# A two-block network on one Trainium2 core: routing spread over two stages, row sums respaced, whole weight loads, tile-wise first units

## The chip, the cores and the metric

The kernel is one program on one core of a Trainium2 chip. The metric is the device time of one execution in microseconds (us). A core has a matrix engine (TensorE, PE in the profile), VectorE (DVE), ScalarE (ACT), GpSimd (POOL) and SyncE (SP), each with its own instruction queue, and 16 DMA engines. Engines wait for each other by semaphores.

## The reference

Two transformer-like blocks for 256 tokens of width 2048, all float32. The part of the first block around which most of the change lies is "peer", a mixture over 16384 experts: eight heads, sixteen experts a head.

```python
q = (hf @ w_q).reshape(T, PEER_HEADS, 2, PEER_DKEY // 2)
s1, s2 = q[:, :, 0] @ sub_k1.T, q[:, :, 1] @ sub_k2.T
v1, i1 = lax.top_k(s1, 16); v2, i2 = lax.top_k(s2, 16)
cand = (v1[..., :, None] + v2[..., None, :]).reshape(T, 8, 256)
sv, si = lax.top_k(cand, 16)
e1, e2 = take_along_axis(i1, si // 16), take_along_axis(i2, si % 16)
expert, gate = e1 * 128 + e2, softmax(sv)
a = gelu(einsum('cd,chkd->chk', x, exp_u[expert]))
out = einsum('chk,chkd->cd', gate * a, exp_v[expert])
```

Before it come adaLN conditioning, a state-space mixer and sparse attention; after it the second block (projections "z", "gate", "abc", "w_o", and a feed-forward "up" and "down"). A root-mean-square norm stands ahead of the peer_q, z and up projections.

## The kernel before, in words

All dense weights stream through `ring` as 333 units of 128 x 4096 float32 (2 MB), in the order of `STREAM`: early (68), w_out, peer_q (8 each), then u0, u1, v0, u2, v1, u3, v2, v3 (16 each), z (17), gate (24), abc, w_o (8), up, down (32). The unit is the clock of the program: positions inside u0 to v3 are counted 0 to 127 (u0 is 0 to 15, v0 32 to 47, v3 112 to 127).

From `SPLIT_0` on each float32 unit is split into two float16 parts: SyncE loads it into one of two raw slots, ScalarE's `hi` writes the high part, VectorE's `low` (line 1149) the rest, each for the first half (p0) and the second half (p1) of the unit. TensorE does three float16 matmuls (lines 570 to 572) a tile. The semaphores are `hi_done`, `split_half` (p0 split), `split_done` (p1 split), `half_used` and `w_used` (TensorE is through with the first half, the unit). `hi` for unit n + 2 starts when unit n's half is used. Before, SyncE loads a unit in two halves of 1 MB: the first waits for `split_half` of two units earlier, the second for `split_done`.

The experts are computed in two ways. For tokens 48 to 255 all experts are evaluated densely in four quarters: u-stages give the activations, and 13 route steps a quarter turn gates into a table by one-hot products. A step is `route` on TensorE (32 small matmuls), and on VectorE `gated` (line 1683), `hot` for the step after next (lines 1669, 1671, 1675) and `gated_low` (line 1689). Quarter 0 is routed in u1, 1 in v0, 2 in v1, 3 in v2; each must be done before its v-stage (v0, v1, v2, v3). For tokens 0 to 47, GpSimd gathers the rows of `exp_u` and `exp_v` with indirect DMAs, 1 MB each: 48 row sums on VectorE (`row_dot`, line 1617) and 48 row products on TensorE (line 623). `DOT_AT` and `PRODUCT_AT` give their positions; `DOT_AT` is spread evenly from 19 to 111. u rows have one buffer, so a gather waits for the sum before it; at each eighth sum 1 MB of activations is loaded too (`h_load`).

`select` turns the sixteen best keys into experts by look-ups: for both index lists a compare, a multiply and a sum over 8 x 16 x 16 = 2048 elements (lines 1562, 1565, 1567), in u0 and at the start of u1.

At the end of w_out, v3 and w_o stands a norm. TensorE sums squares (`stat_sum`, `two_sums`), ScalarE takes the root, VectorE the reciprocal, and `norm_split` gives the sixteen tiles of `h_act` one after the other. The first unit of the next stage runs on these tiles: `unit_a(..., before=...)` waits for tile k in its first half m = 0, then does the second half m = 1.

## Time and profile before

| | |
|---|---|
| median of three runs | 3316.49 us (3311.57 to 3316.68) |
| profiled execution | 3314.53 us |
| its span on the core | 3312.8 us |
| mean granted TensorE clock | 0.979 |
| read from HBM | 814.00 MB |

The span runs from the first to the last instruction. The rows further down are copied from the trace of the profiled execution; a row "A <- B" of a waits view means that engine A stood idle until B ended.

### The profile page before, as it was taken

How to read it: one execution, taken by the hardware profiler on the slowest of the kernel's cores; microseconds unless marked ns; L12 is line 12 of the kernel's file. 1: busy time of each engine (PE TensorE's matmuls, PEld its weight loads, DVE VectorE, ACT ScalarE, POOL GpSimd, SP SyncE). 2: the span in 40 equal slices, each digit the busy share in tenths (PEclk: the TensorE clock that was granted, in tenths of full speed). 3: DMA queues.
4: the chain of work that ended last, by engine and by line, in shares of the span. 5: the costliest groups of instructions: out<-in, count | busy, mean ns of one | idle time of the engine just before them, and what ended most of it. 6: DMA issues, size and time to landing. Idle time of an engine off the chain costs nothing.

```text
span 3312.8 us, 71370 instructions
## 1 busy us (share of the span) xinstructions
PE 3177.2 (96%) x31258; PEld 2827.9 (85%) x31258; DVE 2345.1 (71%) x2673; ACT 1253.7 (38%) x1132; POOL 378.0 (11%) x284
## 2 busy tenths in 40 slices
PE   7999999999899998999899999999999999999998
PEld 4777768799898997889899997888888788888887
DVE  8496145699999985698679876578667665555554
ACT  2000143444444344344444444444443444433332
POOL 0276000000011222122222100200000000000000
PEclk8899999999999999999999999999999999999999
DMA  9657795446577888888998875655555466566663
GB/s 411 248 208 307 292 378 218 156 179 234 196 274 280 322 302 350 288 305 314 349 318 316 339 268 186 201 194 201 194 200 198 171 202 198 199 202 202 203 200 116
DMA packets 105300, 821.55 MB, mean 248 GB/s; under 512 B 12394, under 2 KB 14458, under 8 KB 15552
## 3 DMA queue, kind: packets, MB, share of 16 engines
q1 hardware_dynamic: 86112, 700.49, 58.7%
q0 software_dynamic: 16656, 115.53, 9.1%
q8 instruction: 192, 3.15, 0.4%
q10 hardware_dynamic: 2304, 2.10, 0.2%
q14 instruction: 36, 0.29, 0.0%
HBM read 814.00 MB, written 4.06 MB: 247 GB/s over the span
## 4 chain that ended last, share of the span: by engine, by line
PE 66%; DVE 22%; DMA 7%; issue 3%; ACT 1%; POOL 0%; ACTq 0%; DVEq 0%; SPq 0%
PE psW L570 17%; PE psW L571 16%; PE psW L572 16%; DVE ring L1149 9%; PE psW L568 7%; DMA arena<-urow_dram,rs 4%; DVE arena L1617 2%; DMA ring<-wst_dram 2%; PE psM L694 1%; PE psW L694 1%; DVE arena L1671 1%; PE psM L848 1%; DVE dyn L1675 1%; DVE work L1675 1%; DMA proj<-vrow_dram,rs 1%
## 5 line engine op out<-in xcount | busy, mean ns | idle before, releaser
L1149 DVE SCALAR_TENSOR_TENSOR ring<-ring 128x2048 f16<-128x2048 f32 x526 | 1199.4, 2290 | 516.2 <-ACT ring L1976 514.6
L570 PE MATMUL psW<-h_act,ring 128*128 128x256 f16 (+1 forms) x5088 | 1356.7, 267 | 48.7 <-DVE ring L1149 29.6
L571 PE MATMUL psW<-h_act,ring 128*128 128x256 f16 (+1 forms) x5088 | 1356.6, 267 | 0.0
L572 PE MATMUL psW<-h_act,ring 128*128 128x256 f16 (+1 forms) x5088 | 1356.2, 267 | 0.0
L1976 ACT ACTIVATE ring<-ring 128x2048 f16<-128x2048 f32 x526 | 998.2, 1906 | 868.5 <-PE psW L572 728.1
L570 PE MATMUL psW<-arena,ring 128*128 128x208 f16 (+1 forms) x3072 | 798.1, 260 | 12.1 <-DVE ring L1149 9.3
L571 PE MATMUL psW<-arena,ring 128*128 128x208 f16 (+1 forms) x3072 | 797.8, 260 | 0.0
L572 PE MATMUL psW<-arena,ring 128*128 128x208 f16 (+1 forms) x3072 | 797.7, 260 | 0.0
L570 PEld LDWEIGHTS psW<-h_act,ring 128*128 128x128 f16 x5088 | 500.9, 98 | 116.9 <-DVE ring L1149 40.9
L572 PEld LDWEIGHTS psW<-h_act,ring 128*128 128x128 f16 x5088 | 502.1, 99 | 36.8
L571 PEld LDWEIGHTS psW<-h_act,ring 128*128 128x128 f16 x5088 | 501.3, 99 | 35.3
L570 PEld LDWEIGHTS psW<-arena,ring 128*128 128x128 f16 x3072 | 300.9, 98 | 51.8 <-DVE ring L1149 19.2
L571 PEld LDWEIGHTS psW<-arena,ring 128*128 128x128 f16 x3072 | 301.1, 98 | 11.9
L572 PEld LDWEIGHTS psW<-arena,ring 128*128 128x128 f16 x3072 | 301.1, 98 | 11.9
L568 PE MATMUL psW<-h_act,ring 128*128 128x256 f32 x896 | 202.8, 384 | 2.7 <-DVE h_act L1299 2.7
L568 PEld LDWEIGHTS psW<-h_act,ring 128*128 128x128 f32 x896 | 168.9, 191 | 32.2 <-issue 7.8
L2371 POOL DMA_INDIRECT arena<-urow_dram,rs x48 | 119.9, 2497 | 659.7 <-DVE rs L1617 657.9
L2197 ACT ACTIVATE arena<-work 128x512 f16<-128x512 f32 x52 | 32.8, 630 | 336.4 <-DVE work L1683 336.4
L1617 DVE CUSTOM_DVE_ANT_0 arena<-arena,proj 128x2048 f32<-128x2048 f32 x48 | 109.7, 2285 | 53.6 <-DMA arena<-urow_dram,rs 53.6
L2371 POOL DMA_INDIRECT proj<-vrow_dram,rs x48 | 88.2, 1838 | 87.6 <-PE psM L623 75.4
L694 PE MATMUL psW<-ring,csilu 128*32 128x256 f32 x832 | 64.3, 462 | 23.0 <-DVE small L1260 17.4
L694 PEld LDWEIGHTS psW<-ring,csilu 128*32 128x32 f32 x832 | 29.0, 128 | 51.8 <-issue 33.0
(391 smaller groups left out, 2531.3 us busy)
## 6 DMA issues: line engine op xcount, KB each, us to landing
ring<-wst_dram SPq DMA_DIRECT2D x522, 1024.0 KB
ring<-wst_dram SPq DMA_DIRECT2D x72, 2048.0 KB, 11.3
proj<-h_rows POOLq DMA_DIRECT2D x6, 1024.0 KB
x_res<-xT_dram POOLq DMA_DIRECT2D x2, 2048.0 KB, 17.6
out_dram<-x_res SPq DMA_DIRECT2D x4, 512.0 KB, 2.9
bias_rows<-proj POOLq DMA_DIRECT2D x1, 1536.0 KB, 21.9
x_res<-cmat_dram POOLq DMA_DIRECT2D x1, 1024.0 KB, 5.1
x_res<-bmat_dram ACTq DMA_DIRECT2D x8, 128.0 KB, 3.9
```

What stands on the lines that cost most here:

```text
L568: return nc.tensor.matmul(out, ring[:, w0:w0 + P], rhs, start=first, stop=last)
L570: nc.tensor.matmul(out, whi(s, col, P), xh, start=first, stop=False)
L571: nc.tensor.matmul(out, whi(s, col, P), xl, start=False, stop=False)
L572: return nc.tensor.matmul(out, wlo(s, col, P), xh, start=False, stop=last)
L694: mm = nc.tensor.matmul(ada_bank(n)[32 * c:32 * c + 32, 0:256], csilu[:, k:k + 1].to_broadcast([P, 32]), ring[:, s * UNIT + k * 256:s * UN ...
L848: mm = nc.tensor.matmul(psM[:, 2, 0:T], ring[:, s * UNIT + t * 512 + m * P:s * UNIT + t * 512 + (m + 1) * P], tiles(J, t), start=(t == 0), ...
L1149: ins = stt(wlo(s, c, n), ring[:, s * UNIT + c:s * UNIT + c + n], WSCALE, whi(s, c, n), ALU.mult, ALU.subtract)
L1617: v.tensor_tensor_reduce(row_buf[buf], row_buf[buf], h_rep, 1.0, 0.0, ALU.mult, ALU.add, dots[:, g, h:h + 1]).then_inc(dot_done, 1)
L1671: tt(hot2[b], iota16.unsqueeze(1).to_broadcast([P, STEP_T, P]), cols(1, P), ALU.is_equal).then_inc(hot2_ready, 1)
L1675: ins = tt(hot1[b][:, :, r, :], first1, gate, ALU.mult)
L1976: act(whi(s, p2 * (UNIT // 2), UNIT // 2), ring[:, c], ACT.Copy, scale=WSCALE).then_inc(hi_done, 1)
L2371: g.indirect_dma_start(row_buf[buf], None, (urow_d if kind == "u" else vrow_d)[:, :], bass.IndirectOffsetOnAxis(ap=row_index[:, i:i + 1], ...
```

## The change

1. `ROUTE_AT` and `route_steps` now give (quarter, step) by stage. Quarters 0 and 3 stay in u1 and v2. Quarter 1 takes positions 33 to 62 (v0 and u2), quarter 2 takes 65 to 94 (v1 and u3). Route steps by stage: v0 7, u2 6, v1 7, u3 6, where they were 13, 0, 13, 0.
2. `DOT_AT` starts at 22, goes on by 2.1, by 1.6 between 32 and 96, and by 3.0 after each eighth. It begins 22, 24, 26, 28, 30, 32, 34, 35, 38, 40, 41, 43, 45, 46, 48, 49, 52. Row sums by stage: u1 5 (7 before), v0 9 (8), u2 9 (8), v1 9 (9), u3 9 (8), v2 7 (8). The products follow.
3. The look-ups are done for ranks 0 to 7 over 8 candidates and for ranks 8 to 15 over 16.
4. From unit 72 on each unit is one DMA of 2 MB that waits for `split_done` of two units earlier.
5. The first unit of peer_q, z and up does both halves tile by tile (`first_unit`), the second into `psM`; `keep_clock` puts 12 and 32 matmuls whose result nobody reads around the sums of squares. The first half of the second unit is split ahead of the norm.

```diff
-ROUTE_AT = [14 * k // (STEPS - 1) for k in range(STEPS)]
-
-
-def route_steps(n):
-
-    return [k for k, at in enumerate(ROUTE_AT) if at == n]
-
-
 ORDER = ["u0", "u1", "v0", "u2", "v1", "u3", "v2", "v3"]
 
 
-DOT_AT = [19 + (i * (111 - 19)) // (ROWS_T - 1) for i in range(ROWS_T)]
+
+
+def route_at():
+
+    places = [range(16, 31), list(range(33, 48)) + list(range(48, 63)), list(range(65, 80)) + list(range(80, 95)), range(96, 111)]
+    return [(q, k, units[(len(units) - 1) * k // (STEPS - 1)]) for q, units in enumerate(places) for k in range(STEPS)]
+
+
+ROUTE_AT = route_at()
+
+
+def route_steps(name, n):
+
+    return [(q, k) for q, k, at in ROUTE_AT if at == 16 * ORDER.index(name) + n]
+
+
+def dots_at():
+
+    out, at = [], 22.0
+    for i in range(ROWS_T):
+        out.append(int(at))
+        at += 3.0 if i % HEADS == HEADS - 1 else 1.6 if 32 <= at < 96 else 2.1
+    return out
+
+
+DOT_AT = dots_at()
...
-            def load_halves(u, s, rank):
-
-                for p2, free in enumerate((split_half, split_done)):
-                    c = slice(p2 * HALF, (p2 + 1) * HALF)
-                    sp.wait_ge(free, rank - 1)
-                    sp.dma_start(ring[:, s * UNIT + p2 * HALF:s * UNIT + (p2 + 1) * HALF],
-                                 wst[u, :, c] if isinstance(u, int) else wst[u, :, c].rearrange("o p n -> (o p) n"))\
-                      .then_inc(raw_full[s][p2], 16)
+            def loads(a, b, free, less):
+
+                if a % 2:
+                    sp.wait_ge(free, a - less)
+                    load(a, 1)
+                    a += 1
+                with sp.Fori(a // 2, b // 2) as i:
+                    for s in range(2):
+                        sp.wait_ge(free, i * 2 + (s - less))
+                        sp.dma_start(ring[:, s * UNIT:(s + 1) * UNIT],
+                                     wst[bass.ds(i * 2 + s, 1), :, :].rearrange("o p n -> (o p) n"))\
+                          .then_inc(slot_full[s], 16)
+                if b % 2:
+                    sp.wait_ge(free, b - 1 - less)
+                    load(b - 1, 0)
...
-            n_split = N_UNITS - SPLIT_0
-            with sp.Fori(1, n_split // RAW) as i:
-                for s in range(RAW):
-                    load_halves(bass.ds(i * RAW + (SPLIT_0 + s), 1), (SPLIT_0 + s) % RAW, i * RAW + s)
-            if n_split % RAW:
-                load_halves(N_UNITS - 1, (N_UNITS - 1) % RAW, n_split - 1)
+            loads(SPLIT_0 + 2, N_UNITS, split_done, SPLIT_0 + 1)
...
+            def keep_clock(name, times):
+
+                s = slot_ready(FIRST[name], 0, 0)
+                pe_.wait_ge(split_done, unit_rank[0])
+                for _ in range(times):
+                    nc.tensor.matmul(psM[:, 1, 0:T], whi(s, 0, P), whi(s, 0, T), start=True, stop=True)
+
+            def first_unit(s, before):
+
+                pe_.wait_ge(split_done, unit_rank[0])
+                for k in range(KT):
+                    pe_.wait_ge(h_tile, before + k + 1)
+                    for m, out in enumerate((psW[:, 0, 0:T], psM[:, 0, 0:T])):
+                        mm = product(out, s, m * HALF + k * P, h_split(k), k == 0, k == KT - 1)
+                        if k == KT - 1 and m == 0:
+                            mm.then_inc(half_used, 1)
                 return mm
...
             stage("w_out", from_h, first=2, drained=False)
+            keep_clock("peer_q", 12)
             stat_sum(3)
+            keep_clock("peer_q", 32)
             pe_.wait_ge(bank_free, FIRST["peer_q"] + 4)
...
-                unit_a(s, j % 4, h_split, before=None if j else 0).then_inc(w_used, 1)
+                (unit_a(s, j % 4, h_split) if j else first_unit(s, 0)).then_inc(w_used, 1)
...
-                        route(STEPS * (q + 1) + step_n)
+                    for r, k in route_steps(f"v{q}", n):
+                        route(STEPS * r + k)
...
+                        for r, k in route_steps(f"u{q + 2}", n):
+                            route(STEPS * r + k)
...
+            keep_clock("z", 12)
             two_sums()
-            stage("z", from_h, head=lambda s, j: unit_a(s, j, h_split, before=KT))
+            keep_clock("z", 32)
+            stage("z", from_h, head=lambda s, j: first_unit(s, KT))
...
+            keep_clock("up", 12)
             stat_sum(7)
-            stage("up", from_h, head=lambda s, j: unit_a(s, j, h_split, before=2 * KT))
+            keep_clock("up", 32)
+            stage("up", from_h, head=lambda s, j: first_unit(s, 2 * KT))
...
-                if j < 7:
-                    low(SPLIT_0 + j, parts=(0,))
+                low(SPLIT_0 + j, parts=(0,))
                 residual_w_out(j)
                 add_squares(3, "w_out", j)
                 if j < 7:
                     low(SPLIT_0 + j, parts=(1,))
...
-            low(SPLIT_0 + 7)
+            low(SPLIT_0 + 7, parts=(1,))
...
+                ranks = ((low8, slice(0, half), half), (high8, slice(half, TOPK), TOPK))
                 for f in range(2):
 
-                    step(tt(cand, partf[:, f, :, :].unsqueeze(3).to_broadcast([P, HEADS, TOPK, TOPK]),
-                            io16.to_broadcast([P, HEADS, TOPK, TOPK]), ALU.is_equal))
+                    for one, k, w in ranks:
+                        D.put(tt(one, partf[:, f, :, k].unsqueeze(3).to_broadcast([P, HEADS, half, w]),
+                                 io16[:, :, :, 0:w].to_broadcast([P, HEADS, half, w]), ALU.is_equal))
+                    D.wait()
                     yield
-                    step(tt(cand, cand, idxf[:, :, f, :].unsqueeze(2).to_broadcast([P, HEADS, TOPK, TOPK]), ALU.mult))
+                    for one, k, w in ranks:
+                        D.put(tt(one, one, idxf[:, :, f, 0:w].unsqueeze(2).to_broadcast([P, HEADS, half, w]), ALU.mult))
+                    D.wait()
                     yield
-                    step(v.tensor_reduce(pick[:, f, :].rearrange("p (h k) -> p h k", h=HEADS), cand, AX_X, ALU.add))
+                    for one, k, w in ranks:
+                        D.put(v.tensor_reduce(pick[:, f, :].rearrange("p (h k) -> p h k", h=HEADS)[:, :, k], one, AX_X, ALU.add))
...
                     low(v0 + n + 2, parts=(0,))
                     residual_v(q - 1, n)
-                    steps = route_steps(n)
                     low(v0 + n + 2, parts=(1,))
-                    for k in steps:
-                        gated(q, k)
-                        hot(q, k + 2)
-                        gated_low(q, k)
+                    for r, k in route_steps(f"v{q - 1}", n):
+                        gated(r, k)
+                        hot(r, k + 2)
+                        gated_low(r, k)
                     rows(f"v{q - 1}", n)
                 if q < 3:
                     for n in range(16):
                         low(FIRST[f"u{q + 1}"] + n + 2)
+                        for r, k in route_steps(f"u{q + 1}", n):
+                            gated(r, k)
+                            hot(r, k + 2)
+                            gated_low(r, k)
                         rows(f"u{q + 1}", n)
...
-                    if split_rank(u) >= RAW:
-                        a.wait_ge(raw_full[s][p2], i * 32 + 16 * (split_rank(u) // RAW))
-                    elif p2 == 0:
+                    if p2 == 0:
                         a.wait_ge(slot_full[s], i * 32 + 16 * n)
...
-                act(A[:, j * 512:(j + 1) * 512], psW[:, j % 4, :], ACT.Copy, scale=1 / WSCALE).then_inc(bank_free, 1)
+                if j:
+                    act(A[:, j * 512:(j + 1) * 512], psW[:, j % 4, :], ACT.Copy, scale=1 / WSCALE).then_inc(bank_free, 1)
+                else:
+                    act(tiles(A, 0), psW[:, 0, 0:T], ACT.Copy, scale=1 / WSCALE)
+                    act(tiles(A, 1), psM[:, 0, 0:T], ACT.Copy, scale=1 / WSCALE).then_inc(bank_free, 1)
```

The same replacements stand in the routing loops of ScalarE, and for z and up in the places that answer to those shown for peer_q.

How the instructions stand, on VectorE, in v0 from its first unit on, before. `L1695` adds a unit's result to `x_res`, `L1149` is a half split, `L1617` a row sum, the rest a route step.

```order
L1695 SCALAR_TENSOR_TENSOR x_res<-psW,mod,x_res 128x208
L1149 SCALAR_TENSOR_TENSOR ring<-ring 128x2048
L1683 SCALAR_TENSOR_TENSOR work<-psM,arena 128x512
L1669 TENSOR_TENSOR work<-dyn,work 128x512
L1671 TENSOR_TENSOR proj<-dyn,work 128x2048
L1675 TENSOR_TENSOR dyn<-work,cbias 128x16x32 x2
L1689 TENSOR_TENSOR arena<-work,arena 128x32x16
L1617 ISA arena,rs<-arena,proj 128x2048
L1617 ISA rs 128x1
L1149 SCALAR_TENSOR_TENSOR ring<-ring 128x2048
L1695 SCALAR_TENSOR_TENSOR x_res<-psW,mod,x_res 128x208
L1149 SCALAR_TENSOR_TENSOR ring<-ring 128x2048
```

The same place in the changed kernel; there `L1747` adds the result, `L1192` splits, `L1669` is the row sum and `L1735` opens a route step.

```order
L1747 SCALAR_TENSOR_TENSOR x_res<-psW,mod,x_res 128x208
L1192 SCALAR_TENSOR_TENSOR ring<-ring 128x2048
L1669 ISA arena,rs<-arena,proj 128x2048
L1669 ISA rs 128x1
L1192 SCALAR_TENSOR_TENSOR ring<-ring 128x2048
L1747 SCALAR_TENSOR_TENSOR x_res<-psW,mod,x_res 128x208
L1192 SCALAR_TENSOR_TENSOR ring<-ring 128x2048
L1735 SCALAR_TENSOR_TENSOR work<-psM,arena 128x512
L1721 TENSOR_TENSOR work<-dyn,work 128x512
L1723 TENSOR_TENSOR proj<-dyn,work 128x2048
L1727 TENSOR_TENSOR dyn<-work,cbias 128x16x32 x2
L1741 TENSOR_TENSOR arena<-work,arena 128x32x16
```

The route step of the first unit is gone, and only the second has one.

VectorE in u2 before, with a row sum for each two units:

```order
L1149 SCALAR_TENSOR_TENSOR ring<-ring 128x2048 x4
L1617 ISA arena,rs<-arena,proj 128x2048
L1617 ISA rs 128x1
L1149 SCALAR_TENSOR_TENSOR ring<-ring 128x2048 x4
L1617 ISA arena,rs<-arena,proj 128x2048
```

and now (`L1735` to `L1741` are a route step):

```order
L1192 SCALAR_TENSOR_TENSOR ring<-ring 128x2048 x2
L1735 SCALAR_TENSOR_TENSOR work<-psM,arena 128x512
L1721 TENSOR_TENSOR work<-dyn,work 128x512
L1723 TENSOR_TENSOR proj<-dyn,work 128x2048
L1727 TENSOR_TENSOR dyn<-work,cbias 128x16x32 x2
L1741 TENSOR_TENSOR arena<-work,arena 128x32x16
L1669 ISA arena,rs<-arena,proj 128x2048
L1669 ISA rs 128x1
L1192 SCALAR_TENSOR_TENSOR ring<-ring 128x2048 x4
```

A route step now stands in every second or third unit of u2, ahead of the row sum.

TensorE from the last matmuls of w_out to the first of peer_q, before. `L676` are the sums of squares.

```order
L571 MATMUL psW<-h_act,ring 128x256
L572 MATMUL psW<-h_act,ring 128x256
L676 MATMUL psM<-work,ones 128x256 x4
L570 MATMUL psW<-h_act,ring 128x256
L571 MATMUL psW<-h_act,ring 128x256
L572 MATMUL psW<-h_act,ring 128x256
L570 MATMUL psW<-h_act,ring 128x256
```

and now, with the fillers (`L608`), and the first unit's halves in turn for each tile (`psW` the first, `psM` the second):

```order
L590 MATMUL psW<-h_act,ring 128x256
L608 MATMUL psM<-ring 128x256 x12
L712 MATMUL psM<-work,ones 128x256 x4
L608 MATMUL psM<-ring 128x256 x32
L588 MATMUL psW<-h_act,ring 128x256
L589 MATMUL psW<-h_act,ring 128x256
L590 MATMUL psW<-h_act,ring 128x256
L588 MATMUL psM<-h_act,ring 128x256
L589 MATMUL psM<-h_act,ring 128x256
L590 MATMUL psM<-h_act,ring 128x256
```

Twelve fillers came ahead of the sums, 32 behind them, and a tile is now followed by six matmuls instead of three.

## Rows read from the trace of the kernel before

**Rows 1.** The page, busy time by engine: us, share of the span, instructions.

```profile
PE 3177.2 (96%) x31258; PEld 2827.9 (85%) x31258; DVE 2345.1 (71%) x2673; ACT 1253.7 (38%) x1132; POOL 378.0 (11%) x284
```

**Rows 2.** Windows by stage (u0, u1, v0, u2, v1, u3): busy us, clock, DMA.

```profile
core 0: us, PE busy (x) PEld busy (x) DVE busy (x) ACT busy (x) POOL busy (x), PEclk, DMA share, GB/s
...
720.00:879.00 159.00, 147.93 (x1609) 145.70 (x1609) 152.04 (x278) 76.98 (x61) 0.56 (x1) 0.97 0.60 213
879.00:1048.00 169.00, 155.61 (x1960) 152.41 (x1958) 166.33 (x137) 73.29 (x62) 29.04 (x11) 0.95 0.69 251
1048.00:1211.00 163.00, 157.56 (x2015) 149.52 (x2014) 157.50 (x143) 65.69 (x46) 36.28 (x17) 0.99 0.85 317
1211.00:1372.00 161.00, 150.11 (x1606) 140.09 (x1604) 95.33 (x53) 68.87 (x50) 32.27 (x19) 0.97 0.93 341
1372.00:1545.00 173.00, 158.81 (x2024) 150.68 (x2023) 160.70 (x145) 66.86 (x47) 38.35 (x17) 0.99 0.80 293
1545.00:1704.00 159.00, 149.29 (x1595) 139.22 (x1593) 93.58 (x53) 67.63 (x49) 30.00 (x19) 0.97 0.92 334
```

**Rows 3.** Waits of TensorE, 720 to 1048: us in total, times, longest.

```profile
PE psW L570 <- DVE ring L1149: 18.3, 6, 5.0
```

**Rows 4.** Waits of VectorE, 653 to 1048.

```profile
DVE arena L1617 <- DMA arena<-urow_dram,rs: 2.5, 1, 2.5
```

**Rows 5.** Waits of TensorE, 1048 to 1704.

```profile
PE psW L570 <- DVE ring L1149: 19.5, 7, 7.2
PE psM L623 <- DMA proj<-vrow_dram,rs: 15.3, 5, 5.6
PE psM L623 <- DVE h_act L1628: 5.4, 2, 2.7
```

**Rows 6.** Waits of VectorE, 1048 to 1704.

```profile
DVE ring L1149 <- ACT ring L1976: 98.4, 45, 8.2
DVE arena L1617 <- DMA arena<-urow_dram,rs: 50.4, 7, 14.2
```

**Rows 7.** The chain in order of time: start us, us, what.

```profile
751.59 4.49 DVE ring L1149 x2
759.76 4.49 DVE ring L1149 x2
...
1209.02 10.80 DMA arena<-urow_dram,rs
...
1223.40 27.11 DMA arena<-urow_dram,rs
```

**Rows 8.** A window of u0 in which TensorE never waits.

```profile
814.00:868.00 54.00, 54.00 (x609) 54.00 (x607) 50.46 (x96) 28.23 (x21) 0.00 (x0) 1.00 0.61 219
```

**Rows 9.** Timeline of VectorE, one route step: start us, us, what.

```profile
893.35 0.69 DVE L1683 SCALAR_TENSOR_TENSOR work<-psM,arena 128x512 f32<-128x512 f32 x1
...
898.56 2.29 DVE L1149 SCALAR_TENSOR_TENSOR ring<-ring 128x2048 f16<-128x2048 f32 x1
```

**Rows 10.** Groups of VectorE by shape: busy us, mean ns, idle before.

```profile
L1562 DVE TENSOR_TENSOR proj<-proj,iota 128x2048 f32<-128x2048 f32 x4 | 9.2, 2289 | 0.1
...
L1812 DVE TENSOR_TENSOR x_res<-x_res,arena 128x1024 f32<-128x1024 f32 x1 | 1.2, 1224 | 0.0
```

**Rows 11.** Timelines of TensorE, VectorE and ScalarE in the pause before peer_q.

```profile
609.89 1.13 PE L676 MATMUL psM<-work,ones 128*128 128x256 f32 x4 [0.83 <-DVE work L1201]
615.57 0.37 PE L570 MATMUL psW<-h_act,ring 128*128 128x256 f16 x1 [4.55 <-DVE h_act L1476]
...
624.84 1.27 DVE L1476 SCALAR_TENSOR_TENSOR h_act<-work,mod,h_act 128x256 f16<-128x256 f32 x3
...
631.95 0.60 ACT L2189 ACTIVATE arena<-psW 128x512 f32<-128x512 f32 x1 [3.27 <-PE psW L572]
```

**Rows 12.** A window in that pause: us, TensorE busy, granted clock, DMA share, GB/s.

```profile
614.60:621.40 6.80, 5.83 (x23) 0.50 0.01 2
```

**Rows 13.** DMA issues (KB, us to landing), and a window with 2 MB loads alone.

```profile
ring<-wst_dram SPq DMA_DIRECT2D x72, 2048.0 KB, 11.3
...
arena<-urow_dram,rs POOLq DMA_INDIRECT x48, 11.5
...
50.00:100.00 50.00, 0.94 (x1) 0.75 1.01 427
```

More of the change, by code:

```diff
@@ L430, in program @@
         slot_full = [sem(f"slot_full{i}") for i in range(RING)]
-        raw_full = [[sem(f"raw_full{i}{half}") for half in ("a", "b")] for i in range(RAW)]
         hi_done, split_done, lanes_ready, tab_ready = sem("hi_done"), sem("split_done"), sem("lanes_ready"), sem("tab_ready")
@@ L2011, in his @@
                 turns = n // 4 - last
+                if head:
+                    body(0)
                 if turns > 1:
-                    with a.Fori(0, turns) as i:
+                    with a.Fori(1 if head else 0, turns) as i:
                         body(i)
```

53 lines of the change are left out of this document (31 added, 22 removed).

## Prediction

> **What bounds the kernel now.** I read the page first: TensorE is busy for 96% of the span [rows 1]. So little can be won by making anything else cheaper as such; what can be won are the stretches in which TensorE waits or runs slowly. Next the stage windows, whose bounds are the ends of the stages' last weight units, rounded to the microsecond [rows 2]. After 2024 TensorE is never idle for long, except in the pause before "up". The losses lie in u0 to v2. A unit of 96 matmuls on 208 columns takes 54.0 / 609 x 96 = 8.5 us where nothing disturbs it [rows 8], so sixteen take 136; the six windows of rows 2 last 159 to 173.
>
> From the waits I then see two different bounds.
> - 653 to 1048 (end of peer_q, u0, u1): VectorE is the bound. TensorE waits 18.3 us for its weight splits from 720 on [rows 3], while VectorE itself stops in 395 us for only 2.5 us, for one gathered row [rows 4].
> - 1048 to 1704 (v0, u2, v1, u3): TensorE waits 19.5 + 15.3 + 5.4 = 40.2 us [rows 5], and VectorE stands for 50.4 us before row sums whose gather hasn't landed and 98.4 us for ScalarE [rows 6]. The work is badly mixed: VectorE is busy 157.5 of 163 us in v0 and 160.7 of 173 in v1, but 95.3 of 161 in u2 and 93.6 of 159 in u3 [rows 2]. And the DMA engines are 93% and 92% busy in u2 and u3. The long gathers (27.1 us at 1223) stand at the head of a group of eight row sums, where the group's activations are loaded too; one alone takes 10.8 us [rows 7].
>
> **The change, part by part.** The sum is made against the profiled execution (3314.5 us, span 3312.8); the median of the timed runs is 3316.5, which is 2 more, and I carry differences over to it. TensorE's necessary work is the same before and after, apart from 132 filler matmuls that lie in pauses. So every gain is a wait or a slow-clock stretch that goes.
>
> *Routing of quarters 1 and 2 over two stages.* One step costs VectorE 898.56 - 893.35 = 5.2 us [rows 9]. Six steps leave v0 and v1 and go to u2 and u3, one row sum (2.3 us) comes to v0 and u3 and one to u2. VectorE's load becomes: v0 157.5 - 31.2 + 2.3 = 129, u2 95.3 + 31.2 + 2.3 = 129, v1 160.7 - 31.2 = 130, u3 93.6 + 31.2 + 2.3 = 127. TensorE needs, for all four, the windows less the waits: 656 - 40 = 616. The granted clocks 0.99, 0.97, 0.99 and 0.97 [rows 2] mean 13 us of lost work, of which I take 3 to lie in waits, so 606 are needed, 151 to 153 each. VectorE is then at 85% in all four and no longer a bound. It keeps the cost of waits for gathers.
>
> *Row sums respaced.* A group's head now comes 3 units (26 to 28 us) after the sum before it, instead of 2 (17 to 19). Against a landing of 20 to 27 us that removes most of the waits at group heads, with which the 7.2 us and similar waits of TensorE go. On the other side, 12 neighbours in these stages now stand one unit apart (34 and 35, 40 and 41, ...). The one buffer for u rows is refilled only after the sum before; landing takes 10.8 [rows 7] to 11.5 us [rows 13], a unit 8.5 to 9.5 and the sum itself 2.2 of it, so VectorE will wait some 4 us at each, 48 us in all. It has (606 - 515) = 91 us of room, and weights are split up to one unit ahead, so TensorE should feel perhaps a tenth: 5 us. Of today's 40.2 us of waits I leave 20 (group heads 2, the v rows of rows 5 about half or 7, the 5.4 for row weights 4, neighbours 5, rest 2), and half of the 10 us of slow clock. Gain of the four stages 20 + 5 = 25, at best 45, at worst 5, if the gathers collide as before.
>
> *u0 and u1.* Here VectorE is the chain, so what it no longer does comes off one for one. Two row sums leave u1 (-4.6), the first two neighbours no longer stand one unit apart, which ends the wait of 2.5 [rows 4], and each of the 12 look-up passes becomes a pass over 512 and one over 1024 elements. 2048 elements take 2289 ns, 1024 take 1224 [rows 10], so 512 some 690; pair 1.9, saved 0.38 each, 4.6 us. Sum 11.7.
>
> *Whole weight transfers.* One load of 2 MB now waits until both halves of the slot are split; before, the first half left one split (2.2 us) and the work between the splits earlier. A 2 MB load lands after 4.9 us at least (at 427 GB/s [rows 13]) and 11.3 us in the crowd of the early stages; I take 7.5 alone, 10 beside gathers. In a stage bound by TensorE a unit's first half must be split 3 units after the last unit on the same split buffer ended: 25.5 us, less 4.1 for the split that frees the slot, less the load, less 4.1 for the next: 7 to 10 us of slack, so cost 0. In u0 VectorE's light units follow each other every 8.2 us, 751.59 to 759.76, with the splits at both ends of the 8.1 us of work [rows 7]. Two units then need load 7.5 + ScalarE 1.9 + 8.1 = 17.5 instead of 16.4: 3 us over six light units. So u0 and u1 gain 11.7 - 3 = 9, between 4 and 12. What comes back: the engines move 427 GB/s at full share with 16 KB packets against 341 / 0.93 = 367 in u2 [rows 13, 2], so the four stages, which now need some 345 GB/s each, run at about 87% share instead of 93%. That supports the 20 us above; I add nothing for it.
>
> The Trainium skill weighs both ways here. DMA: Bandwidth & Descriptors, section Rules for kernel authors, says to overlap by issuing early and waiting late, which halves did better; the same page's Bandwidth section lets larger transfers run nearer to the peak. By the first rule alone the merging would cost; that is the rival D below.
>
> *Tile-wise first units and fillers.* In the pause before peer_q the first matmul runs at 615.57 and the unit is taken at 631.95; VectorE gives the last tile at 626.1 [rows 11]. Before, 48 matmuls (5.2 us) remained after the last tile. Now both halves run per tile, 6 x 0.109 = 0.65 us against a tile every 0.79 us, and since the last three tiles come in a burst the unit ends some 1.5 us after 626.1: 627.6. But 12 fillers stand ahead of the two sums, 1.3 us where 0.83 us were free, so the chain starts some 0.4 us later. Gain 631.95 - 627.6 - 0.4 = 3.9 us; z and up have the same shape: 11.7 in all. The next unit's first half is now split before the norm, so TensorE doesn't stand there.
>
> The clock decides whether that holds. From 614.6 to 621.4 it was at half, that is 1.2 GHz, after TensorE had done nothing from 611.0 on [rows 11, 12]. At that level six matmuls take 1.3 us, longer than a tile, and the gain would be 2.2 us instead of 3.9, 5 us less over three pauses. The 32 fillers (3.5 us) cover the idle 4.55 us but for 1, so I expect full clock.
> TensorE: Matmul & The Clock Gate in the Trainium skill (Part 1, What's actually happening) says that activity releases the throttle; by it the fillers work and the sum keeps the 11.7.
>
> *v2 and v3.* v2 loses one row sum; 1 to 2 us.
>
> Sum: 25 + 9 + 11.7 + 1.5 = 47, so 3316.5 - 47 = 3269.
>
> **Rivals.**
> - A (50%): as above, 3258 to 3280.
> - B (22%): the gathers stay the bound of v0 to u3. For it: 92 and 93% DMA share, 50 us of VectorE's waits, and the neighbours one unit apart. The four stages gain 5 and u0/u1 6: 3316.5 - 5 - 6 - 11.7 - 1 = 3293.
> - C (20%): with VectorE at 85% and cheaper packets nearly all waits go: 45 + 12 + 11.7 + 2 = 71, 3246.
> - D (6%), slower: the merged load becomes the pace. It decides where two units' time (2 x 9.4) is less than load + 1.9 + 4.4, thus from a load of 12.5 us on. Were 2 MB to take the 20 us and more of the worst gathers throughout the 64 units of v0 to u3, each would take (20 + 6.3) / 2 = 13.2 us, 3.7 more, +240 us; at 14 us +0.7 a unit, +45 us and in the end some 3320 to 3330. Against it: 1 MB gathers of the same kind land in 11.5 us with their share of the crowd.
> - E (2%): nothing is won, 3316: only if waits merely change their names.
>
> **How the numbers follow.** The forecast is A's, 3269. The range takes A and most of B and C: 3243 to 3294. Two runs of this kernel differ by up to 5 us, 0.15%, so a change under 0.2% (6.6 us) can't be told from none. Faster by more: A, B, C, less a little for a B that goes on: 0.91; same 0.03; slower 0.06.
>
> **What would show it.** Right: v0 and v1 about 153 to 158 us, u2 and u3 154 to 160; VectorE busy near 129 in all four; u1 near 161; the three pauses each 3.5 to 4 us shorter with granted clock 1.00 throughout; no wait of VectorE over 10 us for a gather. Wrong: waits of ScalarE for the weight ring that grow from a few microseconds to more than 8 and are followed by waits of TensorE for the weight split (rival D); VectorE waiting over 60 us for gathers in v0 to u3 (rival B); a slow clock in the pauses (5 us less).

## The result and the profile after

The changed kernel takes 3327.25 us (median of six runs, 3322.18 to 3333.97), the kernel before 3311.82 us on the same chip: ratio 1.0041, 95% interval 1.0027 to 1.0055. It is slower by 0.4%; the forecast was 3269 us. Its profiled execution has a span of 3323.3 us. The page's busy time by engine answers to [rows 1]:

```profile
PE 3179.2 (96%) x31390; PEld 2836.0 (85%) x31390; DVE 2341.2 (70%) x2685; ACT 1252.8 (38%) x1135; POOL 362.1 (11%) x284
```

The cause is not to be seen there. TensorE is busy for 2 us more, although its 132 fillers alone take 15.4 us, so the total hides what moved. The stage windows show it. Those of [rows 2] are bounded one unit late, so both kernels are cut anew here, at the ends of the stages' last units. Columns as in [rows 2]; first the kernel before, v0, u2, v1, u3, v2:

```profile
1037.90:1202.80 164.90, 158.04 (x2019) 149.99 (x2019) 159.41 (x143) 65.72 (x47) 39.93 (x18) 0.99 0.84 309
1202.80:1363.60 160.80, 149.91 (x1603) 139.90 (x1601) 99.11 (x58) 68.95 (x49) 33.38 (x19) 0.97 0.93 343
1363.60:1536.10 172.50, 158.31 (x2018) 150.18 (x2017) 156.22 (x140) 65.67 (x47) 39.22 (x18) 0.99 0.80 292
1536.10:1695.80 159.70, 149.99 (x1602) 139.93 (x1601) 96.61 (x56) 68.82 (x49) 29.29 (x17) 0.97 0.93 338
1695.80:1853.10 157.30, 156.11 (x2016) 148.53 (x2014) 151.12 (x134) 65.04 (x46) 40.13 (x17) 1.00 0.83 309
```

and the changed kernel, the same five:

```profile
1028.40:1183.90 155.50, 150.31 (x1783) 144.10 (x1784) 125.92 (x104) 64.10 (x40) 30.77 (x17) 0.99 0.89 324
1183.90:1359.30 175.40, 157.23 (x1836) 145.68 (x1836) 130.50 (x95) 70.49 (x55) 38.99 (x21) 0.94 0.85 318
1359.30:1521.90 162.60, 154.51 (x1806) 143.81 (x1803) 132.59 (x109) 64.54 (x41) 33.41 (x18) 0.98 0.88 326
1521.90:1690.10 168.20, 156.10 (x1833) 145.22 (x1829) 121.04 (x89) 69.18 (x55) 40.49 (x21) 0.96 0.87 308
1690.10:1871.80 181.70, 158.53 (x2009) 149.90 (x2008) 160.08 (x140) 69.18 (x49) 31.34 (x14) 0.94 0.75 289
```

VectorE's load is level now, as meant (126, 131, 133, 121 us), and v0 and v1 are 9.4 and 9.9 us shorter. But u2, u3 and v2 are 14.6, 8.5 and 24.4 us longer. Waits from the start of v0 to the end of v2, the kernel before and then the changed one, in one column order (who waits, for whom: us in total, times, longest):

```profile
ACT ring L1976 <- DMA ring<-wst_dram: 74.1, 27, 10.2
DVE arena L1617 <- DMA arena<-urow_dram,rs: 51.1, 8, 14.2
PE psW L570 <- DVE ring L1149: 20.7, 8, 7.2
PE psM L623 <- DMA proj<-vrow_dram,rs: 15.3, 5, 5.6
```

```profile
ACT ring L2027 <- DMA ring<-wst_dram: 240.8, 51, 15.3
PE psM L659 <- DMA proj<-vrow_dram,rs: 47.5, 7, 17.6
DVE arena L1669 <- DMA arena<-urow_dram,rs: 27.8, 11, 5.5
PE psM L659 <- DVE h_act L1680: 11.2, 3, 5.8
PE psW L588 <- DVE ring L1192: 5.1, 3, 3.8
```

Two rows grew most. TensorE waits 47.5 us for v rows instead of 15.3, and ScalarE 240.8 us for weights instead of 74.1. VectorE's waits for u rows, which the new positions were to shorten, did fall (27.8 us instead of 51.1). In the chain that ended last, which had no weight load between 100 us and the end of v2 before, pieces like these stand (start, us from issue to landing, what):

```profile
744.69 7.62 DMA ring<-wst_dram
...
1227.73 25.20 DMA proj<-vrow_dram,rs
...
1385.82 18.22 DMA ring<-wst_dram
...
1526.32 27.68 DMA proj<-vrow_dram,rs
...
1674.69 32.84 DMA proj<-vrow_dram,rs
```

GpSimd's timeline around the last of them shows what it waited behind (start, us, operation, idle before and its end):

```profile
1672.45 0.65 POOL L2441 DMA_DIRECT2D proj<-h_rows  x1 [11.30 <-DVE rs L1669]
1673.40 0.99 POOL L2436 DMA_INDIRECT arena<-urow_dram,rs  x1 [0.30 <-issue]
1674.69 2.84 POOL L2436 DMA_INDIRECT proj<-vrow_dram,rs  x1 [0.30 <-issue]
1681.74 0.94 POOL L2436 DMA_INDIRECT proj<-vrow_dram,rs  x1 [4.21 <-PE psM L659]
1707.81 0.94 POOL L2436 DMA_INDIRECT arena<-urow_dram,rs  x1 [25.13 <-DVE rs L1669]
```

A group's activations, its first u row and two v rows, 4 MB, are asked for within 9.3 us. The v row of 1674.69 lands 32.84 us later; in the kernel before a v row takes 13.0 us (median from v0 to v2, longest 14.9 of the landings that can be read). There no v row is asked for right behind a group's head, its first u row, as at 1546.89:

```profile
1546.89 0.65 POOL L2376 DMA_DIRECT2D proj<-h_rows  x1 [11.64 <-DVE rs L1617]
1547.85 1.83 POOL L2371 DMA_INDIRECT arena<-urow_dram,rs  x1 [0.30 <-issue]
1574.66 2.77 POOL L2371 DMA_INDIRECT arena<-urow_dram,rs  x1 [24.98 <-DVE rs L1617]
```

The kernel before isn't quick at its heads either: at 1223.40 the u row took 27.11 us [rows 7], with 2 MB asked for. So a long landing goes with a head in both kernels; what is new is that v rows, for which TensorE waits, have it too.

The tables explain this. `ROW_LOADS` sorts u gather i at `DOT_AT[i-1] + 0.9` and v gather i at `PRODUCT_AT[i-2] + 1.0`. Around the head u40, before: v33 94.0, u40 95.9, u41 97.9, v34 98.0. Now: u40 92.9, v33 93.0, v34 95.0, u41 95.9. In the changed kernel three of the five heads in v0 to v2 have a v gather 0.1 unit behind them (u16, u32 and u40), and these are the three v rows in the chain above; before there was none.

The three pauses (at the starts of peer_q, z and up), before and after; the column behind POOL is the granted clock:

```profile
608.20:631.90 23.70, 17.04 (x106) 9.97 (x106) 21.80 (x42) 11.88 (x19) 0.00 (x0) 0.86 0.10 31
2001.30:2023.40 22.10, 15.80 (x102) 9.68 (x103) 21.15 (x41) 11.04 (x20) 0.00 (x0) 0.85 0.13 41
2617.70:2640.30 22.60, 15.88 (x107) 9.82 (x106) 20.80 (x38) 10.68 (x19) 0.00 (x0) 0.85 0.11 34
```

```profile
602.80:622.60 19.80, 18.75 (x150) 14.08 (x149) 16.98 (x37) 10.33 (x19) 0.00 (x0) 1.00 0.04 18
2019.30:2037.40 18.10, 17.35 (x146) 13.26 (x145) 16.21 (x40) 9.43 (x20) 0.00 (x0) 1.00 0.14 60
2631.70:2650.70 19.00, 18.01 (x151) 14.08 (x149) 15.80 (x36) 9.08 (x19) 0.00 (x0) 1.00 0.04 16
```

3.9, 4.0 and 3.6 us shorter, 11.5 in all.

### The profile page after: what moved, and what is told of

The parts are those of the page before. It is cut to its first block, busy times and chain, and to the rows that moved or that the text cites. A ratio compares the mean times of both kernels' runs of the same rounds, so it can differ in the third digit from the quotient of the medians.

```text
span 3323.3 us, 70770 instructions
## 1 busy us (share of the span) xinstructions
PE 3179.2 (96%) x31390; PEld 2836.0 (85%) x31390; DVE 2341.2 (70%) x2685; ACT 1252.8 (38%) x1135; POOL 362.1 (11%) x284
## 4 chain that ended last, share of the span: by engine, by line
PE 64%; DVE 17%; DMA 13%; issue 4%; ACT 2%; POOL 0%; ACTq 0%; DVEq 0%; SPq 0%; POOLq 0%
PE psW L588 16%; PE psW L590 16%; PE psW L589 16%; DVE ring L1192 7%; DMA ring<-wst_dram 7%; PE psW L586 7%; DMA proj<-vrow_dram,rs 3%; DMA arena<-urow_dram,rs 2%; DVE arena L1669 1%; ACT ring L2027 1%; PE psM L730 1%; PE psW L730 1%; PE psM L884 1%; DVE proj L1723 1%; PE psM L659 1%
## 5 line engine op out<-in xcount | busy, mean ns | idle before, releaser
L1192 DVE SCALAR_TENSOR_TENSOR ring<-ring 128x2048 f16<-128x2048 f32 x526 | 1200.5, 2293 | 580.4 <-ACT ring L2027 578.5
L588 PE MATMUL psW<-h_act,ring 128*128 128x256 f16 (+1 forms) x5040 | 1339.0, 266 | 25.3 <-DVE ring L1192 20.5
L589 PE MATMUL psW<-h_act,ring 128*128 128x256 f16 (+1 forms) x5040 | 1338.1, 265 | 0.0
L590 PE MATMUL psW<-h_act,ring 128*128 128x256 f16 (+1 forms) x5040 | 1338.0, 265 | 0.0
L588 PEld LDWEIGHTS psW<-h_act,ring 128*128 128x128 f16 x5040 | 495.1, 98 | 88.7 <-DVE ring L1192 26.4
L590 PEld LDWEIGHTS psW<-h_act,ring 128*128 128x128 f16 x5040 | 495.4, 98 | 34.9
L589 PEld LDWEIGHTS psW<-h_act,ring 128*128 128x128 f16 x5040 | 495.4, 98 | 34.5
L2436 POOL DMA_INDIRECT arena<-urow_dram,rs x48 | 104.4, 2175 | 664.1 <-DVE rs L1669 662.3
L1669 DVE CUSTOM_DVE_ANT_0 arena<-arena,proj 128x2048 f32<-128x2048 f32 x48 | 110.0, 2291 | 27.8 <-DMA arena<-urow_dram,rs 27.8
L2254 ACT ACTIVATE arena<-work 128x512 f16<-128x512 f32 x52 | 32.8, 630 | 238.3 <-DVE work L1735 231.6
L659 PE MATMUL psM<-proj,h_act 128*24 128x512 f32 x384 | 57.0, 668 | 59.9 <-DMA proj<-vrow_dram,rs 47.5
## 6 DMA issues: line engine op xcount, KB each, us to landing
ring<-wst_dram SPq DMA_DIRECT2D x333, 2048.0 KB, 11.5
```

The costliest lines, as they stand in the source:

```text
L588: nc.tensor.matmul(out, whi(s, col, P), xh, start=first, stop=False)
L589: nc.tensor.matmul(out, whi(s, col, P), xl, start=False, stop=False)
L590: return nc.tensor.matmul(out, wlo(s, col, P), xh, start=False, stop=last)
L659: mm = nc.tensor.matmul(psM[32 * c:32 * c + BATCH_T, 2 + i // BATCH_T, :], row_w[:, 8 * (g % 4) + h, :], row_buf[buf][:, 512 * c:512 * c + ...
L1192: ins = stt(wlo(s, c, n), ring[:, s * UNIT + c:s * UNIT + c + n], WSCALE, whi(s, c, n), ALU.mult, ALU.subtract)
L1669: v.tensor_tensor_reduce(row_buf[buf], row_buf[buf], h_rep, 1.0, 0.0, ALU.mult, ALU.add, dots[:, g, h:h + 1]).then_inc(dot_done, 1)
```

## The experiments

Each result is a median with its ratio to the kernel before on the same chip in the same session (3313.8 to 3316.8 us) and the 95% interval. Differences between versions are taken from the ratios (0.0010 is 3.3 us), since the sessions differ a little. Such a difference carries both intervals, 6 to 9 us together; the stage times of single profiles are used beside it where they are steadier (u0 takes 148.4 or 148.5 us in eleven of them). "Halves" are the two 1 MB loads a unit of the kernel before.

**One part of the change undone.** e1_halves: `load_halves` and the `raw_full` waits as before.

```diff
-            loads(SPLIT_0 + 2, N_UNITS, split_done, SPLIT_0 + 1)
...
+                    load_halves(bass.ds(i * RAW + (SPLIT_0 + s), 1), (SPLIT_0 + s) % RAW, i * RAW + s)
```

> The changed kernel with the weight transfers in halves again. In the changed kernel's profile u2, u3 and v2 are 15, 9 and 24 us longer than before, and TensorE waits there for v rows (longest 17.6 us) that landed 25 to 33 us after their issue, each time when a group's activations, its first u row and two v rows stood in the queue together. Theory X, the burst: the new positions put the v gathers right behind a group's head, the form of the weight loads matters little: 3320 to 3330, long landings and waits stay. Theory Y, whole transfers: 16 KB weight packets and later loads crowd the 8 KB row packets: 3285 or less, and ScalarE's waits for weights fall from 48 to 64 us a stage back to 6 to 27.

3309.4 us, 0.9975 (0.9965 to 0.9985): 22 us below the changed kernel, more than X said, less than Y. TensorE still waits 37.1 us for v rows. So both hold in part. By stages, u0 and u1 give 15.7 us of it (148.4 and 162.3 us in e1, 157.1 and 169.3 in the changed kernel; here and below u0 is taken from its first weight matmul on, every other stage from the end of the one before), and v0 to v3 8.6 together.

e2_old_dots:

```diff
-DOT_AT = dots_at()
+DOT_AT = [19 + (i * (111 - 19)) // (ROWS_T - 1) for i in range(ROWS_T)]
```

> The changed kernel with the old DOT_AT (evenly from 19 to 111), and so the old products and gather order. Theory X (burst at a group's head, caused by the new positions): the first products of a group have 5 to 6 units from release to use again instead of 3 to 4, TensorE's waits for v rows fall to the 15 us of before, and 3270 to 3290 results. Theory Y (whole transfers): still 3310 or more. Theory Z (the route steps delay the row sums in u2 and u3): still 3305 or more.

3320.1 us, 1.0012 (1.0000 to 1.0024), 10 us below the changed kernel, where Y and Z had it. The v waits did fall (20.1 us), and u2 to v2 are 36 us shorter in its profile; but u0, u1, v0 and v3 are 25 us longer, v0 alone 11.

e3_old_route:

```diff
-    places = [range(16, 31), list(range(33, 48)) + list(range(48, 63)), list(range(65, 80)) + list(range(80, 95)), range(96, 111)]
+    places = [range(16, 31), range(32, 47), range(64, 79), range(96, 111)]
```

> The changed kernel with quarters 1 and 2 routed in v0 and v1 alone, as before. Theories X and Y: the losses in u2, u3 and v2 stay and v0 and v1 lose their 9 us each: 3335 to 3350. Theory Z (route steps in u2 and u3 make the row sums late, and with them the gathers): 3300 or less.

3338.1 us, 1.0066 (1.0046 to 1.0086). Z falls: the spread routing is a gain, of 8 us here, which is just clear of the noise.

**Parts added one by one.** e4_pauses_lookups undoes all three of these; e5_route_halves adds the routing to it, e6_whole_only the whole transfers.

> The kernel before with only the tile-wise first units, the fillers and the shorter look-ups; weight halves, route and row positions as before. The pauses were 11.5 us shorter in the changed kernel's profile, the look-ups are worth 4.6 us by the prediction's rows: 3300 to 3303 under every theory; 3305 if the look-ups hide nothing of their own.

3293.2 us, 0.9930 (0.9910 to 0.9950), 8 us better than expected.

> Pauses, look-ups and the routing over two stages, with halves and the old DOT_AT: the changed kernel without its whole transfers and without its new positions. By the runs so far halves are worth 18 us, the old positions 7 and the spread routing 11. If the parts add up: 3293 - 11 = 3282, and v0 to v3 10 us shorter than the 962 us of the run with pauses and look-ups alone. If the route steps gain only by covering what whole transfers cost: 3293.

3279.7 us, 0.9892 (0.9875 to 0.9909): the parts add up, and this beats both kernels.

> The run with pauses and look-ups (3293) with whole transfers added and nothing else. If whole transfers cost what they cost beside the new positions: 3293 + 18 = 3311, most of it in u0 and u1, where VectorE is the chain and a unit's first half can no longer come early. If they only hurt beside the new positions (more row gathers at a time): 3293 to 3296. By the prediction's own term: 3 us in u0, 3296.

3333.4 us, 1.0060 (1.0044 to 1.0076): 43 us for the whole transfers alone, twice the dearer expectation. So they cost 40 to 43 us beside the old positions (the 40 from e5 to e2) and 22 beside the new.

**What of a whole transfer costs.** e9_late_both and e10_late_issue start from e4. Both issue the halves late:

```diff
-                for p2, free in enumerate((split_half, split_done)):
+                sp.wait_ge(split_done, rank - 1)
+                for p2 in range(2):
                     c = slice(p2 * HALF, (p2 + 1) * HALF)
-                    sp.wait_ge(free, rank - 1)
```

and e9 makes ScalarE's first half wait for both:

```diff
-                        a.wait_ge(raw_full[s][p2], i * 32 + 16 * (split_rank(u) // RAW))
+                        if p2 == 0:
+                            a.wait_ge(raw_full[s][0], i * 32 + 16 * (split_rank(u) // RAW))
+                            a.wait_ge(raw_full[s][1], i * 32 + 16 * (split_rank(u) // RAW))
```

> The run with pauses and look-ups (3293), its weights still in two 1 MB transfers a unit with 8 KB packets, but both transfers issued only when both halves of the slot are split, and ScalarE starting only when both have landed: the timing of whole transfers without their 16 KB packets. Theory L, the late issue, costs what whole transfers cost (40 us): 3325 to 3335. Theory P, the large packets against the 8 KB packets of the gathers: 3293 to 3300.

3315.0 us, 0.9993 (0.9983 to 1.0003).

> As the run before it in this list, but ScalarE starts a half as soon as that half has landed. Theory L in its strict form (it is the issue that is late): the same 3325 or more. If it is the landing of the last byte that a first half now waits for: about half of the 40 us comes back, 3305 to 3320. Theory P: 3293.

3290.4 us, 0.9921 (0.9906 to 0.9936).

e9 lies between its two theories, and e10 at the price of the packets alone, though e9 shows that they are not all. The late issue costs nothing: e10 is e4. Waiting for the last byte before the first half is split costs 21 to 24 us (e9 against e4 and e10), and 22 more come with one DMA in 16 KB packets (e6). ScalarE's waits for weights don't give the price: from v0 to v2 they are 157.9 us in e10 and 66.1 in e4, at the same time. u0, where no v row is gathered, confirms the first: 148.4 us in e10, 157.1 in e9 and 157.1 in e6. The rest lies where gathers run. From v0 to v2, e6 and then e9, v rows:

```profile
PE psM L659 <- DMA proj<-vrow_dram,rs: 21.7, 5, 6.0
```

```profile
PE psM L658 <- DMA proj<-vrow_dram,rs: 5.0, 2, 3.8
```

That the packets' size does it was not tried by itself (e6 also has one DMA for two). The Trainium skill bears on it in DMA: Bandwidth & Descriptors, section Queues, rings and completion order: a DMA engine takes turns between its queues, and drains a whole packet of one, typically 9 to 17 descriptors, before it goes to the next. If the 16 KB and 8 KB pieces that the profile counts are such descriptors, which no run here shows, a turn of the weight queue is longer with 16 KB, so that gathers come later; the waits of these two runs agree with that.

**The order of the gathers.** e7_v_first (from e1), e11_v_first_old (from e5), e13_after_v_first (the changed kernel) and e14_before_v_first (the kernel before) have one edit:

```diff
-    v = [(PRODUCT_AT[i - V_BUFS] + 1.0 if i >= V_BUFS else PRODUCT_AT[i] - 3.0, "v", i) for i in range(ROWS_T)]
+    v = [(PRODUCT_AT[i - V_BUFS] + 0.8 if i >= V_BUFS else PRODUCT_AT[i] - 3.0, "v", i) for i in range(ROWS_T)]
```

> The changed kernel with halves (3309), in which each v gather's place in GpSimd's queue is 0.2 units earlier, so that at a group's head the first v row goes ahead of the activations and the u row that it followed at 0.1 unit. Theory X1, the order at the head: v rows land in 13 to 16 us instead of 20 to 28, TensorE's 37 us of waits for them fall to 20, 3290. Theory X2, the amount: as much is asked for in as short a time, so the wait moves to VectorE's row sums at the heads and to the second v row: 3303 to 3312. Theory X3: v gathers now block the u gathers when TensorE is late, 3315 or more.

3291.8 us, 0.9927 (0.9912 to 0.9942), as X1 said. From v0 to v2 TensorE has no wait for a v row left:

```profile
PE psW L587 <- DVE ring L1191: 24.7, 15, 5.5
PE psM L658 <- DVE h_act L1679: 11.6, 3, 6.4
PE psW L587 <- DVE arena L1740: 3.6, 2, 2.1
```

A v gather no longer stands behind the u gather of the same unit, which waits for VectorE's row sum (1.0 came after it, 0.8 comes before it). Part of the wait only moved, as X2 said: TensorE waits 24.7 us for splits, 6.8 in e1; all its waits from v0 to v2 fell from 57 to 40 us.

> The fastest version so far (3280: pauses, look-ups, routing over two stages, halves, old DOT_AT) with each v gather 0.2 units earlier in GpSimd's order. With the old positions no v row is asked for beside a group's head, so there is little to win: v waits of TensorE are 16.5 us. If the order matters everywhere: 3270 to 3276. If only at the heads: 3278 to 3282. If v gathers that wait for TensorE hold up u gathers: 3285 or more.

3258.1 us, 0.9817 (0.9803 to 0.9830). My view that the order matters only beside a head was wrong: 25 us, with no v row beside a head before. The tables say why it had to be: a u and a v gather fall on the same unit 20 times with the old positions and 21 times with the new, mostly away from the heads. It is the best version here, 1.8% under the kernel before. Its windows of v0, u2, v1 and u3:

```profile
1018.00:1175.70 157.70, 150.89 (x1798) 142.88 (x1799) 133.80 (x108) 65.29 (x41) 40.87 (x20) 1.00 0.92 350
1175.70:1328.20 152.50, 151.45 (x1828) 143.54 (x1825) 123.45 (x92) 71.30 (x56) 35.71 (x16) 1.00 0.90 344
1328.20:1485.30 157.10, 152.06 (x1800) 143.84 (x1798) 130.39 (x104) 64.88 (x40) 36.57 (x18) 0.99 0.85 318
1485.30:1636.60 151.30, 151.24 (x1823) 143.57 (x1818) 124.28 (x93) 71.38 (x56) 31.32 (x17) 1.00 0.93 356
```

u2 and u3 are TensorE alone, at full clock, and the DMA share is as high as it ever was.

> The changed kernel, whole transfers and new positions included (3327), with each v gather 0.2 units earlier in GpSimd's order and nothing else. The order was worth 18 us beside halves and new positions (3309 to 3292) and 22 us beside halves and old positions (3280 to 3258). If it adds up here too: 3305 to 3310. If whole transfers are by now what sets the pace: 3320 or more.

3287.7 us, 0.9910 (0.9891 to 0.9929): 43 us, twice the expected gain (38 of them from u0 to v3 in the profiles). The landings at the heads stayed as long, up to 32.8 us for a u and 27.3 for a v row, and ScalarE waits even longer for weights (273.4 us); what went are TensorE's waits for v rows, all 47.5 us. With 0.8 for 1.0 the change as made would have been 0.9% faster than before instead of slower.

> The kernel before with this one number changed. If the order in GpSimd's queue was a cost there too: TensorE's 15 us of waits for v rows go and some slow clock behind them, 3296 to 3304. If it pays only where VectorE has room (routing over two stages), since with the old routing VectorE is the bound of v0 and v1: 3310 to 3316.

3297.0 us, 0.9943 (0.9930 to 0.9957): the kernel before paid 19 us for the order too.

e15_v_first_old_route is e11 with the `places` of e3.

> The fastest version (3258) with quarters 1 and 2 routed in v0 and v1 alone. The spread routing was worth 11 to 13 us in three pairs of runs, all with the old gather order. If it stays so: 3270. If the gather order had hidden most of its worth (the prediction expected 25): 3280 to 3285.

3276.6 us, 0.9882 (0.9866 to 0.9898): the routing is worth 22 us here, as much as the second case said.

**Row sums: bunched or dense.** e16, e17 and e18 are e11 with this line of `dots_at` changed (the marks behind the # are mine) and its positions in use again,

```diff
-        at += 3.0 if i % HEADS == HEADS - 1 else 1.6 if 32 <= at < 96 else 2.1
+        at += 4.7 if i % HEADS == HEADS - 1 else 1.6                                                        # e16
+        at += 1.95 if i < 8 or i >= ROWS_T - 9 else 4.8 if i % HEADS == HEADS - 1 else 1.6                  # e17
+        at += 1.78 if 32 <= at < 96 else 2.1                                                                # e18
```

from 19 on in e16 and e17 and from 22 on in e18.

> The fastest version (3258), its row sums as many to a stage as with the old positions (8 in 16 units) but bunched as in the changed kernel: 1.6 units apart, 4.7 after an eighth. The new positions cost 34 us beside the new gather order (3292). They differ in two things: neighbours one unit apart, and 9 row sums and up to 10 products a stage. If the neighbours cost it: 3285 to 3295. If the density does: 3255 to 3265, or less, since a group's head has 4.7 units to land.

3296.4 us, 0.9944 (0.9927 to 0.9960), but of the 38 us between the medians only 6.5 lie in v0 to u3, where its density is the old one.

> The fastest version (3258) with bunched row sums (1.6 units apart, 4.8 after an eighth) in v0 to u3 alone; at both ends the sums are evenly spread as with the old positions. The bunched run (3296) lost only 6.5 us of its 38 in v0 to u3; 9.8 lay in u1, where it has one row sum more, and 27 in v2 and v3. If that reading of its stages holds: 3262 to 3270. If bunching costs wherever it stands: 3280 or more.

3285.2 us, 0.9909 (0.9892 to 0.9925). My reading of e16's stages falls: bunched in the middle alone, it costs 30 us.

> The fastest version (3258) with the row sums of the changed kernel's density (9 in sixteen units instead of 8, by 1.78 units from 32 to 96) but spread evenly, without its gaps of 3 after an eighth. If density is what the new positions cost in v0 to u3 (28 us there with the mended order): 3280 to 3295. If it is the bunching: 3260 to 3268.

3285.7 us, 0.9902 (0.9885 to 0.9920): density without the gaps costs as much, 28 us. What all of them share are sums one unit apart: between 32 and 96 there are 12 pairs in the changed kernel and in e17, 10 in e16, 8 in e18, 1 with the old positions (row sums there, in the order changed kernel, e17, e16, e18, old: 36, 34, 32, 36, 33). VectorE's waits for u rows from v0 to v2 and TensorE's for VectorE's splits, in e11, then in e18, then VectorE's in e7, which has the changed kernel's positions:

```profile
DVE arena L1668 <- DMA arena<-urow_dram,rs: 44.3, 11, 12.1
PE psW L587 <- DVE ring L1191: 10.0, 4, 4.3
```

```profile
DVE arena L1668 <- DMA arena<-urow_dram,rs: 98.0, 15, 15.7
PE psW L587 <- DVE ring L1191: 28.2, 6, 9.5
```

```profile
DVE arena L1668 <- DMA arena<-urow_dram,rs: 78.0, 15, 8.6
```

In e17 it is the row weights that come late (21.6 us instead of 2.5). All of TensorE's waits from v0 to v2 are 16 us in e11 and 40, 41 and 42 us in e7, e17 and e18: VectorE stops for 34 to 54 us more, and TensorE feels 24 to 26 of them. e17, with nearly the old density, speaks for the pairs, e16 with its 6.5 us in v0 to u3 against them alone; how the 28 to 30 us divide stays open.

**Prices of the sure parts.** e8_no_fillers and e12_no_lookups start from e4; the first drops the six `keep_clock` calls, the second has the 2048-element look-ups.

> The run with pauses and look-ups (3293) without the 132 filler matmuls. If the fillers hold TensorE's clock, the three pauses are each 1.5 to 2.5 us longer and the granted clock is at half at the start of peer_q, z and up: 3293 + 5 = 3298 (the prediction's 1.7 a pause). If the clock rises by itself in time: the fillers cost what they take, 3291 to 3293.

3295.5 us, 0.9941 (0.9925 to 0.9958), which can't be told from e4. The pauses can:

```profile
610.90:631.20 20.30, 14.92 (x106) 11.73 (x106) 17.69 (x37) 10.36 (x19) 0.00 (x0) 0.83 0.16 53
1996.60:2016.60 20.00, 14.48 (x103) 11.57 (x104) 18.12 (x41) 9.27 (x20) 0.00 (x0) 0.83 0.17 56
2611.00:2631.30 20.30, 15.17 (x108) 12.00 (x107) 17.06 (x36) 9.32 (x19) 0.00 (x0) 0.83 0.16 52
```

0.5, 1.9 and 1.3 us longer than with fillers, at a clock of 0.83 instead of 1.00: the fillers give 3.7 us of the 11.5.

> The kernel before with the pauses (tile-wise first units and fillers) alone; the run with pauses and look-ups (3293) without its shorter look-ups. The prediction's price of the look-ups, 4.6 us: 3298. By the stages u0 and u1 of the runs so far, about 8 us: 3301. If the pauses were worth less than the 11.5 us that the stages show: above 3305.

3299.3 us, 0.9946 (0.9933 to 0.9960), which by itself can't be told from e4. The profiles can for u0: 151.2 us with the long look-ups, 148.4 with the short ones in e4 and in e8 alike, so 2.8 us. u1 takes 171.9 us with the long ones, and 171.9 in e4 and 170.1 in e8 with the short ones, so 0 to 1.8.

## Why the prediction was wrong, point by point

As percentages of the kernel before, part by part from e4, e5, e1 and the changed kernel: pauses and look-ups -0.70, routing -0.38, new positions +0.83, whole transfers +0.66; in us at 3316, -23, -13, +28, +22. The forecast had the first two right in sign. It put the first at 16.3, too low, and lost the sum on the two others, for which it had put 3 us and, inside its gain of 25, 5 us.

- **Pauses**: forecast 11.7, measured 11.5; the clock stayed at 1.00 as expected. e12 gains 18 us with them alone; 4.6 more lie in u0 to v3 (2.2 of them in u0), and what shortens these stages is not shown.
- **Look-ups**: forecast 4.6 from two durations; 2.8 are shown in u0 and between 0 and 1.8 in u1, where two runs that should be alike (e4 and e8) differ by that much. That VectorE's saving comes off one for one there is not contradicted, and not shown in full.
- **u0 and u1 together**: forecast a gain of 9, measured none (326.5 us before, 326.4 now). The 11.7 us of relief are real: with halves (e1) the two take 310.7 us. Whole transfers took 15.7 of it back, not 3.
- **Routing**: VectorE's level load came out as worked out (129, 129, 130, 127 against 126, 131, 133, 121), but it was worth 13 us of the 25 forecast for it and the row sums together; 22 once the gathers' order no longer took it back.
- **Whole transfers: the first failed step.** "In a stage bound by TensorE ... 7 to 10 us of slack, so cost 0", and 3 us in u0. Measured: 8.7 in u0 and 7.0 in u1 of the changed kernel (e1), 43 in all beside the old positions, 22 beside the new. The step looked for the cost in the later issue, which costs nothing (e10). The cost is that the first half's split, which had begun after 1 MB, now waits for the last byte of 2 MB (21 to 24 us), and a further 22 us that come with the single large DMA, where gathers run; which property of it does that is not shown. In u0 the load was as forecast (7.62 us at 744.69). The slack of the TensorE-bound stages stood on 7.5 to 10 us, while the changed kernel's chain has loads of 18.22 us. Rival D's time, 3320 to 3330, holds the measured one, but that is luck: its load of 14 us throughout didn't occur, TensorE's waits for splits fell, and half of the loss came from the row sums, which D leaves out. What D had right is the place: far below its point of 12.5 us throughout, single units already wait.
- **Row sums respaced: the second failed step.** The text saw the neighbours one unit apart and put VectorE's waits at them at 48 us, of which "TensorE should feel perhaps a tenth: 5 us". Beside halves the new positions cost 28 us with the old order of the gathers (e5 to e1) and 36 with the mended one (e11 to e7); beside whole transfers 10 (from e2). From e11 to e7 VectorE's waits for u rows grew by 34 us, less than forecast, but TensorE's waits grew by 24: the share was wrong, half or more (also in e17 and e18) and not a tenth. In the old order the same loss stood mostly under v rows (37.1 us in e1, 16.5 in e5).
- **The order of the gathers: a term that the sum did not have.** The text never followed "the products follow" into GpSimd's queue. There v33 moved from 1.9 units ahead of the head to 0.1 behind it. But the order is no part of what the new positions cost beside halves, for it cost 25 us with the old positions and 16 with the new, and 19 in the kernel before, where it hid a gain that the forecast did not look for. Only beside whole transfers, in the changed kernel itself, was it worth 43.
- **What the signs said**: v0 in its range, v1, u2 and u3 (162.6, 175.4, 168.2) out of theirs, u1 at 169 instead of 161. The sign "no wait of VectorE over 10 us for a gather" came true (longest 5.5), and B's sign, over 60 us of such waits, stayed away (27.8 in v0 to v2). Both watched u rows only, while the late gathers for which TensorE waited were v rows. The sign given for D, ScalarE's waits for the weight ring of over 8 us, is there (51 waits, longest 15.3); but TensorE's waits for the split behind it fell (5.1 us instead of 20.7). That it was already held up by v rows is my reading.

## What to carry to other kernels

Merging two transfers into one is not free because the bytes are the same: ask when the first consumer may start, and try the late issue and the late landing apart, as e10 and e9 do. When a table of positions moves, write out every queue that is sorted by it, and look who stands behind whom: here the tie between 0.9 and 1.0 unit was worth 16 to 43 us, and 19 in the kernel before. And taking load off one engine pays in full only when what the bound stage really waits for is gone too; the spread routing was worth little more than half (13 us of 22) until the gathers were out of the way. When an engine off the chain is given waits, its share in the bound engine's waits has to be priced from rows, not guessed.

## What the runs showed of the hardware

- A v row of 1 MB lands 13.0 us after its issue in the kernel before (median from v0 to v2), and 25.20, 27.68 and 32.84 us after it at three heads of the changed kernel, where 4 MB are asked for within 7 to 13 us. At a head of the kernel before, with 2 MB asked for, a u row took 27.11 us.
- In u3 the DMA engines carry 356 GB/s at 93% share in e11 and 338 GB/s at 93% in the kernel before, with the same packet sizes. So the share does not tell how much more they could carry.
- Where TensorE waits now and then, its clock is lower too: in u2 and v2 of the changed kernel the granted clock is 0.94, in the same stages of e11 it is 1.00. TensorE's busy time in u2 is 157.23 us against 151.45, with one row product more.
- 44 matmuls of 128x256 in a pause hold the clock at 1.00 where it is 0.83 without them, which shortens the pause by 1.2 us.
